# A two-layer fp32 transformer on one core: the stage boundaries rewritten (x updated on VectorE in merged groups, longer token-half tails, four half-wise first units, shared KV projection inside the third FFN)

## What is computed

```
def rms_norm(x, g):
    xf = x.astype(jnp.float32)
    y = xf * lax.rsqrt(jnp.mean(xf * xf, axis=-1, keepdims=True) + NORM_EPS)
    return (y * g.astype(jnp.float32)).astype(x.dtype)
def swiglu(h, w1, w3, w2):
    return (jax.nn.silu(h @ w1) * (h @ w3)) @ w2
...
    for l in range(DEPTH):
        g = norm_gains[l]
        x = x + 0.5 * rms_norm(swiglu(rms_norm(x, g[0]), ffn_w1[l, 0], ffn_w3[l, 0], ffn_w2[l, 0]), g[1])
        hn = rms_norm(x, g[2])
        ... (mix = moba_mixer(hn) in layer 0, mla_mixer(hn, shared k and v) in layer 1)
        x = x + rms_norm(mix, g[3])
        x = x + 0.5 * rms_norm(swiglu(rms_norm(x, g[4]), ffn_w1[l, 1], ffn_w3[l, 1], ffn_w2[l, 1]), g[5])
        if l == N_A_LAYERS - 1:
            k_nope, k_rope, v_sh = mla_shared_kv(x, kv_in_norm, w_dkv_kr, kv_norm, w_ukv, cos_r, sin_r)
```

## Time and profile before

| | |
|---|---|
| runs | 2040.48, 2041.49, 2043.30 us; median 2041.49 |
| profiled execution | span 2041.5 us from the first to the last instruction; nothing is timed around it |
| busy | TensorE 1961.2, VectorE 1047.7, ScalarE 676.8, GpSimd 145.5 us |
| mean granted TensorE clock | 0.978 of 2.4 GHz |

### The profile page before, as it was taken

One profiled execution on the slowest core, in us unless ns is written; L12 is line 12 of the kernel. 1 busy time (PEld: TensorE's weight loads), 2 busy tenths in 40 slices (PEclk: granted clock), 3 DMA queues, 4 the chain that ended last, 5 costly groups with the idle time before them and its releaser, 6 DMA issues.

```text
span 2041.5 us, 24735 instructions
## 1 busy us (share of the span) xinstructions
PE 1961.2 (96%) x9287; PEld 1634.2 (80%) x9287; DVE 1047.7 (51%) x1529; ACT 676.8 (33%) x1031; POOL 145.5 (7%) x152
## 2 busy tenths in 40 slices
PE   7999999889998999999999999999999989999998
PEld 5888888768887888888878888888777878888887
DVE  5444433667658544442475444335666575444324
ACT  4332222245533323321253223222555333223211
POOL 1000000311103000000120000002100030000002
PEclk8999999989998999999999999999899989999999
DMA  5333332222212233333223333332211213333331
GB/s 156 103 89 96 100 103 86 73 65 80 71 54 83 83 103 91 94 103 95 80 63 103 103 103 85 97 107 57 63 36 53 81 43 91 94 103 93 98 98 42
DMA packets 344626, 174.56 MB, mean 86 GB/s; under 512 B 12159, under 2 KB 344045, under 8 KB 344557
## 3 DMA queue, kind: packets, MB, share of 16 engines
q1 hardware_dynamic: 341728, 171.47, 29.4%
q10 hardware_dynamic: 2828, 2.15, 0.4%
HBM read 171.50 MB, written 2.10 MB: 85 GB/s over the span
## 4 chain that ended last, share of the span: by engine, by line
PE 86%; DVE 8%; ACT 2%; issue 2%; POOL 1%; DMA 1%; SPq 0%; DVEq 0%; ACTq 0%
PE acc L1255 26%; PE acc L1257 26%; PE acc L1256 26%; DVE xT L891 2%; PE sco L1255 2%; PE sco L1257 2%; PE sco L1256 2%; DVE xg L849 2%; DVE wl L814 1%; PE acc L1426 1%; ACT tmp L595 1%; DMA raw<-in_ffn_w_dram 1%; ACT prob_odd L607 1%; DVE mx L983 0%; PE aux L1282 0%
## 5 line engine op out<-in xcount | busy, mean ns | idle before, releaser
L1255 PE MATMUL acc<-xg,wh 128*128 128x512 f32 (+1 forms) x1736 | 679.1, 391 | 33.9 <-DVE xg L849 28.6
L1256 PE MATMUL acc<-xg,wh 128*128 128x512 f32 (+1 forms) x1736 | 667.7, 385 | 0.0
L1257 PE MATMUL acc<-xg,wl 128*128 128x512 f32 (+1 forms) x1736 | 667.4, 384 | 0.0
L814 DVE TENSOR_TENSOR wl<-raw,wh 128x1024 fp32r<-128x1024 f32 (+2 forms) x320 | 372.4, 1190 | 109.5 <-ACT wh L527 105.7
L1255 PEld LDWEIGHTS acc<-xg,wh 128*128 128x128 f32 x1736 | 332.2, 191 | 106.2 <-DVE xg L849 30.8
L1257 PEld LDWEIGHTS acc<-xg,wl 128*128 128x128 f32 x1736 | 332.0, 191 | 63.8
L1256 PEld LDWEIGHTS acc<-xg,wh 128*128 128x128 f32 x1736 | 332.5, 192 | 63.1 <-issue 1.7
L527 ACT ACTIVATE wh<-raw 128x1024 fp32r<-128x1024 f32 x332 | 326.0, 1020 | 113.9 <-PE acc L1257 89.6
L1255 PE MATMUL acc<-hT,wh 128*128 128x512 f32 (+1 forms) x726 | 271.0, 373 | 0.0
L1256 PE MATMUL acc<-hT,wh 128*128 128x512 f32 (+1 forms) x726 | 270.7, 373 | 0.0
L1257 PE MATMUL acc<-hT,wl 128*128 128x512 f32 (+1 forms) x726 | 270.7, 373 | 0.0
(11 more groups left out here) (226 smaller groups left out, 1803.8 us busy)
## 6 DMA issues: line engine op xcount, KB each, us to landing
raw<-in_ffn_w_dram SPq DMA_DIRECT2D x240, 512.0 KB, 4.5
raw<-in_ffn_w_dram SPq DMA_DIRECT2D x32, 384.0 KB, 3.5
raw<-in_moba_w_qkv_dram SPq DMA_DIRECT2D x24, 512.0 KB, 3.9
raw<-in_moba_w_o_dram SPq DMA_DIRECT2D x8, 512.0 KB, 4.1
raw<-in_mla_w_o_dram SPq DMA_DIRECT2D x8, 512.0 KB, 4.3
raw<-in_mla_w_dq_dram SPq DMA_DIRECT2D x4, 512.0 KB, 4.1
raw<-in_mla_w_uq_dram SPq DMA_DIRECT2D x8, 256.0 KB, 3.0
raw<-in_w_ukv_dram SPq DMA_DIRECT2D x16, 128.0 KB, 3.2
```

Source lines behind the costliest of these rows:

```text
L814: v.tensor_tensor(wl[:, slot, 0:tiles], raw[:, slot, 0:tiles], f32(wh[:, slot, 0:tiles]), ALU.subtract).then_inc(w_lo, 1)
L1255: t.matmul(dst, w_h, m_h, start=start, stop=False)
L1256: t.matmul(dst, w_h, m_l, start=False, stop=False)
L1257: return t.matmul(dst, w_l, m_h, start=False, stop=stop)
```

## The change

It keeps the mathematics and rewrites what stands at each boundary:

1. **Evacuation.** ScalarE instead of VectorE reads the output tiles out of PSUM: a Square straight from the bank and a Copy times the norm's gain into `y` (`y_tile`).
2. **Longer tails.** The last two tiles of an FFN (before: one) and the last four of w_o (before: two) are computed by halves of the tokens; in an FFN the third unit of tile 6 and tile 7 for e=1 come after both tiles' first halves. The squares of these tiles are not added on VectorE but each goes into `mean` as a part of its own, so `mean` gets longer.
3. **x update.** GpSimd's products go. VectorE multiplies and adds in groups of 2, 3 and 3 tiles (`x_group`; in the output stage 4 groups of 2), two instructions a group, with the factor read from PSUM.
4. **Four first units by halves.** All four first units run for e=0 and then all four for e=1 (`quad`). GpSimd's `split_two` goes, VectorE makes all low parts.
5. **Squares of x.** Four Squares over 4 tiles by 256 tokens, four adds over 1024 and 512 columns in place of seven adds, and two parts left for `mean`.
6. **KV projection.** The fourth stage is empty; its four units stand behind the first four of the third FFN, over whole rows, and the norm of its result falls into that FFN's next units.

The core of the diff (ScalarE's and SyncE's sides follow the same order):

```
+    stages = [FFN_U, MOBA_U, FFN_U, [], FFN_U[:SLOTS] + KV_U + FFN_U[SLOTS:], MLA_U, FFN_U]
+    TAIL_FFN, TAIL_WO = (KD - 2, KD - 1), (KD - 4, KD - 3, KD - 2, KD - 1)
+    GROUPS, OUT_GROUPS = ((0, 2), (2, 5), (5, KD)), tuple((k, k + 2) for k in range(0, KD, 2))
...
-                    pool.wait_ge(r_ready, EV0[n] + e + 1)
-                    for m in range(1, KD):
-                        g.tensor_tensor(y[:, m, half(e)], y[:, m, half(e)], Rb[:, half(e)], ALU.mult
-                                        ).then_inc(yr_ready, 1)
...
+            def y_tile(m, bank, g_post, cols=slice(0, S)):
+                s.activation(y[:, m, cols], bank[:, cols], COPY, scale=gains[:, g_post + m:g_post + m + 1]
+                             ).then_inc(evacuated, 1)
...
+            def x_group(t, n, e, group, groups, r_end):
+                a, b = groups[group]
...
+                v.tensor_tensor(y[:, a:b, half(e)], y[:, a:b, half(e)],
+                                norm_bank[e][:, half(e)].unsqueeze(1).broadcast_to([P, b - a, HALF]), ALU.mult
+                                ).then_inc(r_ready if last else y_ready, 1)
...
+                v.tensor_tensor(xT[:, a:b, half(e)], xT[:, a:b, half(e)], y[:, a:b, half(e)], ALU.add
+                                ).then_inc(x_ready, 1)
+            def x_update(t, n, factor, gcol, u, r_end):
...
+                post_var(n, 0)
+                post_diag(n, 0, factor)
+                split(u)
+                for e in range(2):
+                    x_group(t, n, e, 0, GROUPS, r_end)
+                    x_group(t, n, e, 1, GROUPS, r_end)
+                    lo(e, 0)
+                    lo(e, 1)
+                    if e == 0:
+                        split(u + 1)
+                    x_group(t, n, e, 2, GROUPS, r_end)
+                    for m in range(2, KD):
+                        if e == 0 and m == 5:
+                            post_var(n, 1)
+                        lo(e, m)
+                    if e == 0:
+                        post_diag(n, 1, factor)
+                        split(u + 2)
+                        split(u + 3)
...
+            def quad(st, xg0, by_halves, n_post, n_pre):
...
+                        if first and (p, k) == (0, 1):
+                            post_mean(n_post, 1)
+                        if first and (p, k) == (1, 1):
+                            post_spread(n_post, 1)
+                        if not first and (p, k) == (1, 2):
+                            mean(n_pre)
+                        if not first and (p, k) == (1, 6):
+                            spread(n_pre)
...
+                for e in range(2 if by_halves else 1):
+                    for p in range(2):
+                        if by_halves and e == 0:
+                            pe.wait_ge(evacuated, r - (LAST[n_post] if p == 0 else 0))
+                        pair(u + 2 * p, (acc[2 * p], acc[2 * p + 1]), xg, xg0 + (KD * e if p == 0 else 0),
+                             half(e) if by_halves else slice(0, S), not by_halves or e == 1, p == 0, among(p, e))
...
+                for s in range(ND - 1):
+                    down(a, s, banks[0][0], half(0))
+                    down(a, s, banks[1][0], half(1)).then_inc(unit_done, 1)
+                down(a, ND - 1, banks[0][0], half(0)).then_inc(half_psum, 1)
...
+                down(a, ND - 1, banks[1][0], half(1),
+                     before=lambda k: post_mean(n_post, 0) if k == 3 else None).then_inc(unit_done, 1)
```

More of the change, by code:

```diff
@@ L1334, in norm_over_two @@
-            def norm_over_two(u, n):
-                unit(u + 2, acc[2][:], from_x(xg))
-                unit(u + 3, acc[3][:], from_x(xg), before=norm_among(n, 0, 4))
-            def shared_norm(k):
-                if k == 0:
-                    mean(N_CKV, width=KVR)
-                if k == 7:
-                    spread(N_CKV, diag=ckv_diag)
-            def ffn(st, xg0, by_halves, after, n_pre, n_post):
-                F0 = KF * FFN_STAGE[st]
-                u, r = U0[st], R0[st]
-                pair(u, (acc[0], acc[1]), xg, xg0, by_halves, after)
-                if st == 4:
-                    unit(u + 2, acc[2][:], from_x(xg))
-                    pe.wait_ge(evacuated, r)
-                    unit(u + 3, acc[3][:], from_x(xg), before=shared_norm)
-                else:
-                    norm_over_two(u, n_pre)
-                with pe.Fori(1, KF // 2) as it:
+                for k in range(UT):
+                    if streamed:
+                        pe.wait_ge(xg_ready, xg0 + k + 1)
+                    for a in range(2):
+                        ins = product(banks[a][:, cols], wh[:, (u + a) % SLOTS, k], wl[:, (u + a) % SLOTS, k],
+                                      buf[:, 0, k, cols], buf[:, 1, k, cols], k == 0, k == UT - 1)
+                        if k == UT - 1 and done:
+                            ins.then_inc(unit_done, 1)
+                    if after is not None:
+                        after(k)
@@ new lines, in shared_kv, with ffn @@
+            def shared_kv():
+                pair(KV_U0, (sco[1], sco[2]), xkv, XG0[X_F1] + 2 * KD, slice(0, S), True, True)
+                pe.wait_ge(r_ready, EV0[N_PRE3])
+                unit(KV_U0 + 2, sco[0][:], from_x(xkv), UT // 2, stop=False)
+                unit(KV_U0 + 3, sco[0][:], lambda k: (xkv[:, 0, UT // 2 + k], xkv[:, 1, UT // 2 + k]), UT // 2,
+                     start=False)
+            def ffn(st, xg0, by_halves, n_last, n_pre, n_post):
+                F0 = KF * FFN_STAGE[st]
+                u, r, first = U0[st], R0[st], 1
+                quad(st, xg0, by_halves, n_last, n_pre)
+                if st == KV_ST:
+                    shared_kv()
+                    u, r, first = u + len(KV_U), r + KK + 1, 2
+                    for a in range(4):
+                        pe.wait_ge(evacuated, R0[st] + a + 1)
+                        if a == 2:
+                            mean(N_CKV, width=KVR)
+                        if a == 3:
+                            spread(N_CKV, diag=ckv_diag)
+                        unit(u + 4 + a, acc[a][:], from_x(xg))
+                with pe.Fori(first, KF // 2) as it:
@@ L1364, in hidden, with down @@
                     return lambda k: (hT[:, 0, UT * s + k, cols], hT[:, 1, UT * s + k, cols])
-                for m in range(KD - 1):
+                def down(m, s, dst, cols=slice(0, S), before=None):
+                    w = d0 + ND * m + s
+                    pe.wait_ge(w_lo, w + 1)
+                    return tiles(dst[:, cols], w % SLOTS, 0, DOWN[s], hidden(s, cols), start=s == 0,
+                                 stop=s == ND - 1, before=before)
+                for m in range(TAIL_FFN[0]):
                     pe.wait_ge(evacuated, r0 + m - 3)
```

642 lines of the change are left out of this document (327 added, 315 removed).

## The result

The changed kernel takes 2004.89 us (median of 4 runs, 2004.04 to 2006.36) beside 2041.22 us before: a ratio of 0.9819 with a 95% interval of 0.9805 to 0.9833, 36.3 us less. The forecast was 2009 us. The profiled execution has a span of 2001.7 us and was timed at 2004.04, so 2.3 us lie outside its span. It is the fastest of the four. The span of 2041.5 us of the kernel before is not its whole time either: all 29 executions of it that were timed beside the experiments have 1.8 or 1.9 us outside their span, so its profiled execution must be the one of 2043.30 us, the slowest.

A forecast was written before the change was run, and what follows sets the result against it. TensorE, busy 96% of the span, was taken to bound the kernel. Seven stretches (+0.9, -4.7, -8.5, -6.3, -3.4, -10.2, 0) sum to -32.2 us, taking 2041.5 to 2009 us; range 2001 to 2023.

The forecast's parts named there:

- The four waits I named: TensorE waits: MoBA's fifth unit 3.1 us, MLA's rope unit 3.0, Rb at w_o 0.75, e=1's third tile 0.85.
- the steps of the prediction: FFN boundary timed from t = 0 after tile 7's first half: next stage at 11.9, four units end at 41.7.
- the stretch: One of seven windows around the boundaries where the change acts on TensorE; the last, the end, was forecast at 50.0 us.
- The pace of the first pairs: After an FFN boundary: 0.79 us a step on x, e=0's first pair ending at t = 19.95, e=1's at 33.5.
- Half clock goes.: At the boundaries: waits and half clock worth 52 us go, while 20 us of work come.
- my 57.2: Each w_o stretch, into the second and the fourth FFN: 57.2 us, against 65.7 and 67.4 before.
- the clock still falls: Rival: half clock stays at the boundaries, priced at 15 us (between 0 and 24), 2024 us; chance 0.17.
- my own sign: At the boundaries: the prediction is wrong if the granted clock is not near 1.
- more falls away: Rival: MLA's and MoBA's heads behind the stretches may spare some 7 us, 2002 us or less; chance 0.06.
- One threshold: VectorE's merged instructions at boundaries: a slow rate decides from 0.5 us per tile on (6.5 a boundary).
- rival on merged instructions: VectorE at boundaries: merged instructions take 0.88 us per tile, not 0.29; five waits of 15, 2084 us; chance 0.04.
- the waits only move: Rival: VectorE at 0.39 us per tile, not 0.29, loses 3 a boundary, 15 in all, 2024 us; chance 0.1.

The follow-up runs named there:

- e7: Changed kernel with the squares of the last tiles but one added on VectorE, so means after a stage have 8 records; 1995.72 us.
- e10: Changed kernel with the edits of e6 and e7 together, shortening both kinds of mean; 1990.93 us.
- e1: Changed kernel with nine unneeded GpSimd products of 256 columns after each power of a boundary; 2015.47 us.
- e4: Changed kernel with each mean of a norm after a stage computed twice; 2040.04 us.
- e8: Changed kernel with MoBA's eighth unit moved ahead of the second head's value transposes on TensorE; 2014.01 us.
- e11: e10 with the low part of MLA's seventh unit and two adds of cq's squares moved behind the first rope unit's products; 1987.49 us.
- e5: Changed kernel with the low part of MLA's seventh unit behind the cq parts on VectorE, not ahead of Rb; 2009.13 us.
- e6: Changed kernel with a third add of the squares of x on VectorE, leaving one part in the means before a stage; 2002.99 us.
- e9: The changed kernel itself, repeated on another chip; 2004.83 us.
- e12: e11 with MoBA's fifth unit in another PSUM bank, so it does not wait for the first rotary product; 1985.39 us.
- e2: Changed kernel with every merged multiply and add of a group as single instructions of one tile; 2010.20 us.
- e3: Changed kernel with the third and fourth unit over all 512 tokens at five boundaries, not by halves; 2027.00 us.

## Why the prediction was right

**Mechanism.** The four waits I named are there with the size I gave: MoBA's fifth unit 2.7 (forecast 3.1), MLA's rope unit 3.2 (3.0), `Rb` at w_o 0.8 (0.75); e=1's third tile 0.7 (0.85). An FFN's boundary keeps to the steps of the prediction: in MoBA's, from t = 0 at 376.43, the next stage starts at 11.8 (forecast 11.9) and the fifth unit at 43.3 (44.8). The merged product takes 0.94 to 0.95; a one-column record 0.105 (0.11); records grow by 712. At the end VectorE stood 6.4 us before the `var` of e=1, with e=0's last groups behind it, at t = 13.9 (forecast 14.0), and the stretch is only 0.6 shorter.

**What was mis-sized.** Four terms.
1. *The pace of the first pairs.* I let e=0's end at t = 19.95. With no wait the steps run at the bare 0.72 and not at 0.79, and it ended at 18.9. The pace is 0.6 of that; by my own terms (mean to 14.9, six more steps of 0.79) it was 19.6, so 0.3 was a slip in adding up. e=1's first pair took 6.7 for 7.3. Together that makes 1.1 to 1.6 at each FFN boundary: MoBA 64.9 for 66.4, MLA 80.0 for 81.6, and KV 1.1 less once the 1.7 behind it are counted. (MLA's 80.0 holds 3.4 us at half clock.) The start is 0.8 shorter than forecast: I kept the half clock that it had before (0.96, about 1 us of cost), and it had none this time, while the longer mean came as forecast.
2. *"Half clock goes."* It did not at w_o: 6.8 and 3.4 us of it stayed (0.94, 0.97), behind means of 20 records. Without it they would have been 55.8 and 56.1, so w_o too was 1.1 to 1.4 below my 57.2. About half of that is a slip: the terms that I wrote down for w_o add up to 56.7 (the wait of 0.75 lies in the 7.2). This is the rival "the clock still falls", true at two of five boundaries and worth about 7 us with MLA's (0.98), not 15. By my own sign, a granted clock near 1 at the boundaries, these two miss. Of the means behind w_o e7 and e10 show that the fall hangs on their length.
3. *The clock behind the stretches.* MLA's loop gained 3.6, the rival "more falls away" at its place. e1 to e4, e8, e10 and e11 lose it again with hardly a change in that code, e5, e6, e7, e9 and e12 do not, so it is no sure property of the change.
4. *The base.* I set the span of 2041.5 equal to the median. With the 1.8 us around it that execution took 2043.30, so the stretches that I started from were those of the slowest of the three runs. By spans -39.8 were measured for -32.2, by medians -36.3.

**What was luck.** Without half clock at w_o and in MLA the stretches would have been some 7 us shorter still, and the forecast 11 off and not 4: the pace and two slips made it too long, the half clock that stayed took much of that back. The mechanism held without luck, the last 4 us did not. One threshold was wrong too: that slow merged instructions decide from 0.5 per tile on leaves out the slack of 2 us a half, which the 75 us for 0.88 take in; with it the threshold is 0.62. It was not reached.

**The slack.** I thought of VectorE as 2 us a half ahead of TensorE and feared slow merged instructions. e1 says that the free GpSimd is worth about 10 us (8 by the stretches), e2 that merging is worth 3 to 4, e3 that the halved third and fourth units are worth 22 (19 by the stretches). My reading, which no run with two of them undone tests: the first two matter only as far as they eat into the cover that the third gives, TensorE's work that waits for nothing of VectorE's. The law of the rival on merged instructions (0.88 per tile beside GpSimd, whatever is merged) was wrong too: the loss is up to 0.4 an instruction and hardly larger for 1024 columns than for 256, and with a factor read from PSUM there is none. The rival "the waits only move" priced merging at 3 us a boundary; e2 shows 0.7.

**The price.** The means in the form of the change cost: e10 gets 13.9 us back with 32 short adds on VectorE. With e11 and e12 the kernel stands at 1985.4, a ratio of 0.9723 (0.9710 to 0.9737) to before.

What stays open: why the clock falls in one kernel's MLA loop and not in the next, and where it fell in the slower executions of e5 and e6, which have no trace. The evacuation by ScalarE and the two-tile tail were not undone by themselves, and nor was the moved KV projection, where waits of 6.0 us went.

## What to carry to other kernels

Count what an engine has to do while it waits for a factor, and give it work that doesn't need it: half-width first units cost 0.04 us a tile and hid nearly 4 us a boundary. Tiny matmuls are not free: a sum over partitions cost 0.105 us for each one-column record here, so add up on an engine with slack first, and look for the granted clock behind a row of them. Before moving a unit to fill a wait, look whether its own buffer is released by what is waited for.
